# A two-layer attention and mixture-of-experts trunk: the input projection reads x before the norm's factor, GpSimd holds the empty scatters, and the heads' operands are split earlier and in three rows

## The reference, cut to what matters

```
h = rms_norm(x, norm1_gain);  z = h @ w_in          # columns q | k | v | u, 512 each
q, k = per-head rms_norm (8 heads of 64), rotary on the first 16 dims, q scaled by 1/8
att  = three causal dilated windows merged by their softmax denominators
pool = four channel groups: causal trailing mean of u over 2/4/8/16 positions minus u, a linear map, a scale
x = x + concat(att, pool) @ w_out
x = x + experts(rms_norm(x, norm2_gain))            # top-1 of 4 groups, top-2 of 4 experts in it
```

## Time and profile before

| | |
|---|---|
| median of 3 runs | 1663.27 us (1661.2 to 1667.27) |
| the profiled execution's own time | 1666.6 us |
| its span, first to last instruction | 1664.8 us |
| mean granted TensorE clock | 0.936 |
| PE / DVE / ACT / GpSimd busy | 1427.9 / 997.0 / 666.1 / 348.0 us |

### The profile page before, as it was taken

How to read it: one execution, slowest core, us unless ns; L and a number is a source line. 1 busy time by engine, 2 the same in 40 slices (tenths; PEclk the granted TensorE clock), 3 DMA queues, 4 the chain that set the end, 5 groups by cost and what they waited for, 6 DMA issues and landing times.

```text
span 1664.8 us, 24259 instructions
## 1 busy us (share of the span) xinstructions
PE 1427.9 (86%) x7323; PEld 1142.5 (69%) x7324; DVE 997.0 (60%) x1919; ACT 666.1 (40%) x1028; POOL 348.0 (21%) x204
## 2 busy tenths in 40 slices
PE   5999978998995699999299999699989938999981
PEld 4887868887784466666178788688968826666650
DVE  6777666664446666666467866756534475556560
ACT  4232145673211355555332313556611124555450
POOL 1000059002000123233510000950100011223324
PEclk9999988999998799999699999989999959999995
DMA  8100020000129599984770001100001665989937
GB/s 313 31 1 0 0 102 2 1 2 13 51 80 371 168 285 298 341 223 101 162 239 0 1 0 65 38 1 1 2 14 75 232 223 163 274 258 311 294 50 127
DMA packets 115873, 204.46 MB, mean 123 GB/s; under 512 B 9816, under 2 KB 76576, under 8 KB 115776
## 3 DMA queue, kind: packets, MB, share of 16 engines
q1 hardware_dynamic: 90976, 130.77, 22.9%
q0 software_dynamic: 19136, 53.67, 14.6%
q10 hardware_dynamic: 5664, 18.88, 2.9%
HBM read 169.72 MB, written 49.28 MB: 132 GB/s over the span
## 4 chain that ended last, share of the span: by engine, by line
PE 60%; DMA 14%; DVE 10%; issue 9%; ACT 4%; DVEq 2%; POOL 1%; ACTq 1%; SPq 0%; POOLq 0%; PEld 0%; PEldq 0%
PE ps L1501 18%; DMA out_x<-x_res,arena 11%; PE ps L1634 9%; PE ps L1481 9%; PE ps L1715 7%; PE ps L1587 7%; PE ps L1730 4%; PE ps L1561 2%; DMA big<-in_w_in 2%; PE ps L1563 1%; PE ps L1651 1%; DVE arena L1262 1%; DVEq L1372 1%; DVE xgT_lo L1376 1%; PE ps L1621 1%
## 5 line engine op out<-in xcount | busy, mean ns | idle before, releaser
L1367 DVE TENSOR_TENSOR gu_lo<-big,gu_hi 128x2048 fp32r<-128x2048 f32 x96 | 218.6, 2291 | 166.4 <-ACT gu_hi L892 133.0
L1481 PE MATMUL ps<-cst,arena 128*128 128x128 f32 x1226 | 183.2, 283 | 75.1 <-DVE arena L1019 32.9
L1481 PEld LDWEIGHTS ps<-cst,arena 128*128 128x128 f32 x1226 | 148.3, 145 | 124.7 <-DVE arena L1019 34.9
L1501 PE MATMUL ps<-w_in_hi,hT_hi 128*128 128x512 f32 x512 | 204.9, 400 | 12.8 <-DVE hT_lo L1037 10.0
L1501 PE MATMUL ps<-w_in_hi,hT_lo 128*128 128x512 f32 x512 | 201.3, 393 | 0.0
L1501 PE MATMUL ps<-w_in_lo,hT_hi 128*128 128x512 f32 x512 | 201.0, 393 | 0.0
L671 POOL DMA_INDIRECT x_res<-token_rows,row_tok x62 | 91.7, 1479 | 516.0 <-issue 308.7
L892 ACT ACTIVATE gu_hi<-big 128x2048 fp32r (+1 forms) x96 | 181.4, 1916 | 35.3 <-PE ps L1715 35.0
L1715 PE MATMUL ps<-gu_hi,xgT_hi 128*128 128x512 f32 x360 | 150.1, 417 | 23.6 <-DVE xgT_lo L1376 23.6
L1730 PE MATMUL ps<-big,arena 128*128 x360 | 163.8, 598 | 4.7 <-issue 4.7
L1156 DVE CUSTOM_DVE_ANT_0 arena<-ps,cst 128x128 f32<-128x128 f32 (+7 forms) x128 | 96.8, 756 | 102.7 <-PE ps L1563 102.2
(11 more groups left out here) (182 smaller groups left out, 2306.2 us busy)
## 6 DMA issues: line engine op xcount, KB each, us to landing
big<-in_w_gate SPq DMA_DIRECT2D x32, 1024.0 KB, 9.2
big<-in_w_up SPq DMA_DIRECT2D x32, 1024.0 KB, 13.9
big<-in_w_down SPq DMA_DIRECT2D x32, 1024.0 KB, 14.0
big<-in_w_in SPq DMA_DIRECT2D x14, 1024.0 KB, 10.1
big<-in_w_out SPq DMA_DIRECT2D x4, 2048.0 KB, 10.4
token_rows<-arena ACTq DMA_DIRECT2D x16, 512.0 KB, 3.2
out_x<-x_res ACTq DMA_DIRECT2D x16, 512.0 KB, 4.0
x_res<-out_x SPq DMA_DIRECT2D x8, 512.0 KB, 5.9
```

Source lines behind the costliest of these rows:

```text
L1367: ve.tensor_tensor(out=gu_lo[i], in0=raw, in1=gu_hi[i].bitcast(f32), op=ALU.subtract)\
L1481: ins = te.transpose(ps[:, bank + i // 4, (i % 4) * P:(i % 4 + 1) * P], src, ident)
L1501: ins = te.matmul(ps[:, 2 + 2 * par_ + i, :], a[par_][:, k, :], b[:, k, :], start=k == 0 and n == 0, stop=k == K - 1 and n == 2)
```

## The change

1. **Projection.** PE transposes x itself (`xr`) as soon as the block is loaded; xs, `norm_x_again` and the multiplication in `norm_x` go. r is kept for each block in st[:, 128 + t] and applied later: ACT's squares of q and k and its copies of v and u take it as a scale, and `norm_qk` multiplies it into its own factor. The order of the first steps changes in both layers: `gain1(0)` comes before `norm_x(0)`. All blocks are written out, not looped over.
2. **Scatters.** ACT no longer waits in its branches. GpSimd's `add_rows(j)` first waits for a new semaphore `may_add`, raised by one behind each `moe_down`, and by 15 for the spare ones: in layer 0 after ACT has split the first quarter of the next w_in and SP has raised `spare_may`, in layer 1 right after the last used block.
3. **Operands.** For the first head, q's high part and low part and the clearing of k_low[0] move into the last block of the projection; k's split is done for 896 and then 128 tokens. For the others, DVE's three instructions are spread over rows 1, 2 and 3. Buffers move so that this is free of conflicts.

```diff
@@ scatters
                 def add_rows(j):
+                    pool.wait_ge(may_add, j + 1)
                     pool.wait_ge(y0_ready, upto(l, BLOCKS, j + 1))
...
+                pool.wait_ge(may_clear, upto(l, 1, 1))
+                pool.sem_inc(s_passed, 1)
+                pool.sem_clear(may_add)
@@ ACT
             def square_x(l, t, par_):
                 a_.wait_ge(x_ready, upto(l, T, t + 1))
-                if not first(t):
-                    a_.wait_ge(xs_ready, upto(l, 2 * T, t))
-                    a_.wait_ge(xt_done, upto(l, 2 * T, t))
+                if t >= 2:
+                    a_.wait_ge(r_ready, upto(l, T, t - 1))
...
+                    if h and last(t, T):
+                        a_.wait_ge(t_evac, upto(l, 3 * T, T))
+                        q_top(0, 0)
                     a_.wait_ge(z_done, upto(l, 4 * T, 2 * n + 1))
-                    sc.activation(sqz, ps[:, 2 + 2 * par_, :].rearrange("p (h c) -> p h c", c=HD), ACT.Square)\
+                    a_.wait_ge(r_ready, upto(l, T, t + 1))
+                    sc.activation(sqz, ps[:, 2 + 2 * par_, :].rearrange("p (h c) -> p h c", c=HD), ACT.Square,
+                                  scale=st[:, 128 + t:129 + t])\
...
                     sc.activation(y[slot][:, 512:1024], ps[:, 5, :], ACT.Copy).then_inc(y1_ready, 1)
+                    a_.sem_inc(may_add, 1)
...
                     with a_.Else():
-                        a_.wait_ge(spare_may, upto(l, 1, 1))
                         a_.sem_inc(y1_ready, 1)
...
-                    in_high(l + 1, 0, [0])
+                    first_gain(l + 1)
+                    in_high(l + 1, 0)
+                    a_.wait_ge(spare_may, upto(l, 1, 1))
+                    a_.sem_inc(may_add, SPARE)
+                    a_.sem_inc(may_clear, 1)
                     square_x(l + 1, 0, 0)
-                    first_gain(l + 1)
-                    in_high(l + 1, 0, [1])
                     in_high(l + 1, 1)
@@ DVE
             def norm_x(l, t, par_):
                 dve.wait_ge(sd1, upto(l, T, t + 1))
-                r = st[:, 4 + par_:5 + par_]
-                rsqrt(st[:, par_:par_ + 1], st[:, 2 + par_:3 + par_], r, st[:, 6:7], 1.0 / D)
-                ve.tensor_copy(st[:, ds(128 + t, 1)], r)
-                ve.tensor_scalar(xs, xr[:, t, :], r, None, ALU.mult).then_inc(xs_ready, 1)
+                rsqrt(st[:, par_:par_ + 1], st[:, 2 + par_:3 + par_], st[:, 128 + t:129 + t], st[:, 6:7], 1.0 / D)
+                dve.sem_inc(r_ready, 1)
...
+            def first_q_low(l):
+                dve.wait_ge(q_high_in, upto(l, 2 * PAIRS, 1))
+                ve.tensor_tensor(out=q_parts[0][HD:P, :], in0=qT[0:HD, 0, :],
+                                 in1=q_parts[0][0:HD, :].bitcast(f32), op=ALU.subtract)
+                dve.wait_ge(z_done, upto(l, 4 * T, 4 * T - 2))
+                ve.memset(k_low[0][HD:P, :].bitcast(f32), 0.0)
...
+                if h and last(t, T):
+                    first_q_low(l)
+                if h == 0 and not last(t, T):
+                    norm_x(l, t + 1, 1 - par_)
...
+            gain1(0, 0, 0)
             norm_x(0, 0, 0)
-            in_low(0, 0, [0])
-            gain1(0, 0, 0)
-            in_low(0, 0, [1])
+            in_low(0, 0)
...
+                for n, c in enumerate((slice(0, SEQ - P), slice(SEQ - P, SEQ))):
+                    k_lower(0, 0, n + 1, c)
+                    ins = k_copy(0, 0, c)
+                ins.then_inc(staged, 1)
                 dve.wait_ge(tqk_done, upto(l, 3 * T, 3 * T))
-                ve.memset(k_low[0][HD:P, :].bitcast(f32), 0.0)
                 ve.memset(k_low[1][0:HD, :].bitcast(f32), 0.0)
-                q_and_k_low(0, 0, 0)
...
-                    if n == 3:
-                        q_and_k_low(p, 1, 2 * p + 1)
-                    if n == 11 and p < PAIRS - 1:
-                        q_and_k_low(p + 1, 0, 2 * p + 2)
+                    a, q = 1 - n // T, p + n // T
+                    if q < PAIRS:
+                        if n % T == 1:
+                            q_low(q, a, 2 * q + a)
+                        if n % T == 2:
+                            k_lower(q, a, 2 * q + a + 2)
+                        if n % T == 3:
+                            k_copy(q, a).then_inc(staged, 1)
...
                 with dve.If(l < DEPTH - 1):
-                    in_low(l + 1, 0, [0])
-                    norm_x(l + 1, 0, 0)
-                    in_low(l + 1, 0, [1])
+                    in_low(l + 1, 0)
                     dve.wait_ge(gain_in, upto(l + 1, 1, 1))
                     gain1(l + 1, 0, 0)
+                    norm_x(l + 1, 0, 0)
@@ PE
                 def xt(n):
-                    pe.wait_ge(xs_ready, upto(l, 2 * T, n + 1))
-                    transposes(0, cols(xs, K)).then_inc(xt_done, 1)
+                    if n < T:
+                        pe.wait_ge(x_ready, upto(l, T, n + 1))
+                    transposes(0, cols(xr[:, n % T, :], K)).then_inc(xt_done, 1)
```

More of the change, by code:

```diff
@@ L310, in trunk @@
         spare_may = sem("spare_may")
+        may_add = sem("may_add")
+        may_clear = sem("may_clear")
         gu_loaded = sem("gu_loaded")
@@ L395, in trunk @@
         SURE = (2 * SEQ // P - 1) // RING
+        SPARE = BLOCKS - 2 * SEQ // P
         def before(slot, m):
@@ L799, in _ @@
                 for h in range(2):
-                    steps(a_, T, lambda t, par_, m: in_act(t, par_, h), ch)
+                    for t in range(T):
+                        in_act(t, t % 2, h)
                     if h == 0:
@@ L1049, in in_low @@
                                      in1=w_in_hi[i % 2][:, c].bitcast(f32), op=ALU.subtract).then_inc(win_split, 1)
+            def first_q_low(l):
[4 more added lines that the diff above has]
+                ve.memset(k_low[0][HD:P, :].bitcast(f32), 0.0)
             def in_dve(l, t, par_, h):
                 n = h * T + t
-                if h == 0:
-                    if not last(t, T):
-                        norm_x(l, t + 1, 1 - par_)
-                    else:
-                        norm_x_again(l, 0)
-                elif not (first(t) or last(t, T)):
-                    norm_x_again(l, t + 1)
+                if h and last(t, T):
+                    first_q_low(l)
+                if h == 0 and not last(t, T):
+                    norm_x(l, t + 1, 1 - par_)
                 if h == 0 or not last(t, T):
@@ L1065, in in_dve @@
                 if h == 0 and last(t, T):
-                    norm_x_again(l, 1)
                     in_low(l, 3)
@@ L1120, in _, with k_lower, k_copy, q_low @@
                 ch.restart()
-                steps(dve, T, lambda t, par_, m: in_dve(l, t, par_, 0), ch, begun=True)
-                steps(dve, T, lambda t, par_, m: in_dve(l, t, par_, 1), ch)
-                def q_and_k_low(p, a, n):
+                for n in range(1, 2 * T):
+                    in_dve(l, n % T, n % 2, n // T)
+                def k_lower(p, a, n, c=slice(0, SEQ)):
+                    own = slice(HD * a, HD * (a + 1))
+                    dve.wait_ge(k_high_in, upto(l, 2 * PAIRS + 1, n))
+                    ve.tensor_tensor(out=k_low[a][own, c], in0=kT[own, p, c],
+                                     in1=k_high[a][own, c].bitcast(f32), op=ALU.subtract)
+                def k_copy(p, a, c=slice(0, SEQ)):
+                    own, other = slice(HD * a, HD * (a + 1)), slice(HD * (1 - a), HD * (2 - a))
+                    return ve.tensor_copy(k_high[a][other, c], kT[own, p, c])
+                def q_low(p, a, n):
                     own, other = slice(HD * a, HD * (a + 1)), slice(HD * (1 - a), HD * (2 - a))
@@ L1131, in q_and_k_low @@
                                      in1=q_parts[a][own, :].bitcast(f32), op=ALU.subtract)
-                    dve.wait_ge(k_high_in, upto(l, 2 * PAIRS + 1, n + 2))
-                    ve.tensor_tensor(out=k_low[a][own, :], in0=kT[own, p, :],
-                                     in1=k_high[a][own, :].bitcast(f32), op=ALU.subtract)
-                    ve.tensor_copy(k_high[a][other, :], kT[own, p, :]).then_inc(staged, 1)
+                for n, c in enumerate((slice(0, SEQ - P), slice(SEQ - P, SEQ))):
+                    k_lower(0, 0, n + 1, c)
+                    ins = k_copy(0, 0, c)
+                ins.then_inc(staged, 1)
                 dve.wait_ge(tqk_done, upto(l, 3 * T, 3 * T))
-                ve.memset(k_low[0][HD:P, :].bitcast(f32), 0.0)
                 ve.memset(k_low[1][0:HD, :].bitcast(f32), 0.0)
-                q_and_k_low(0, 0, 0)
                 dve.wait_ge(s_mask, 16)
@@ L1542, in _ @@
                 for h in range(2):
-                    steps(pe, T, lambda t, par_, m: in_pe(t, par_, h))
+                    for t in range(T):
+                        in_pe(t, t % 2, h)
                 turn(1, T - 1, (T - 1) % 2)
@@ L1774, in maybe_pe @@
                     with pe.Else():
+                        if not last(t, BLOCKS):
+                            pe.wait_ge(xtm_done, upto(l, BLOCKS, t + 1))
```

(3 more changed lines are left out.)

37 lines of the change are left out of this document (17 added, 20 removed).

## The result

The changed kernel takes 1650.84 us, the median of six runs (1639.09 to 1652.59); the kernel before took 1665.27 beside it. The ratio is 0.9887, with a 95% interval of 0.9855 to 0.9920. So it is faster: the medians differ by 14.4 us, and the ratio would make it 18.8. I forecast 35.3 us and a range of 1612 to 1646. The sign was right, and the measured time lies outside the range (by the ratio it would be 1646.5, at its edge). The profiled execution took 1649.49 us, 17.1 less than the profiled one of before.

A forecast was written before the change was run, and what follows sets the result against it. PE bounds the kernel, busy 86% of the span, so gains lie where it stands still or runs at 1.2 GHz. 3.6 + 1.7 + 14 + 12 + 5 - 1 = 35.3 us, from the median 1663.3 to 1628; range 1612 to 1646.

The forecast's parts named there:

- the splits in three rows: Attention heads: spreading DVE's splits makes PE's stalls shorter and keeps its clock up; 12 us, bounds 4 and 18.
- a rival with a chance of 0.06: Attention heads: each split pays its own wait for GpSimd, 19 us more and no gain in the rows; 1659 us.
- a third burst: Layer 1's heads: attention begins 6 us earlier against GpSimd, so another burst of splits falls into pooling; -2.0 us.
- 0.3 us a head: Eight other heads: the gain counted for each from spreading the splits, within the 15.8 us taken as 12.
- Start of layer 0: Projection's start: PE begins matmuls at 15.8 instead of 17.97 and block 1 follows earlier; 3.6 us, 4 at most.
- w_in, which I had named as a rival: Projection's start, both layers: PE still stands behind weights, so 3.6 and 5 us are lost; 1637 us, chance 0.08.
- Middle: Middle of the projection, both layers: dropping norm_x_again saves 0.86 us each; 1.7 us, bounds 1 and 2.5.
- Begin of attention: Both layers: scores come 6.1 us earlier and the clock stays at 1.00; 14 us, bounds 10.5 and 16.
- Between the layers: Passage to layer 1: ACT leaves without its 15.69 us wait, PE's matmuls begin 10 us earlier; 5 us, bounds 2 and 9.
- the pause of 6 us: Passage to layer 1: PE lacks work some 6 us before block 1, falls to 1.2 GHz and loses 2 us.
- GpSimd's wait: Scatters: one more wait for each costs 1 us over 45 used blocks, bounds 0 and 6.

The follow-up runs named there:

- the pieces: The changed kernel with GpSimd's split of the output weights cut into instructions of 1024 elements: 1624.49 us, ratio 0.9771; the same cut in the kernel before: 1662.49 us, 0.9974.

## Why the prediction was wrong

**The step that failed** is the one on the splits in three rows, and in it the sentence that DVE "does the same work", so that the end of the stretch "moves by no more than DVE's idle time in it". The work is not the same, because a split that meets one of GpSimd's instructions lasts until that one ends. I had the mechanism as a rival with a chance of 0.06, and sized it from the earlier trace rows at 2.07 us a split at most, since before no split met more than the tail of GpSimd's longest one; the copy in head 2 paid 8.26 - 0.69 = 7.57. So the two heads 2, where I had counted on 1.5 us, lost 18.2. For layer 1 I let a third burst fall into pooling, for 2 us, but I never asked which instruction of GpSimd each split would meet after attention had moved by 9.9 us and GpSimd by 3.8. GpSimd's order in attention is fixed and its instructions were in the trace of before; laying the heads' new times over it would have shown the 9 us subtraction under head 2. The instruction's length and its position were each varied, and both agree: the copy grows with the piece (1.76, 3.97, 8.27 us), and moving the long instruction away gives the same as cutting it (0.9777 and 0.9771). With it cut the kernel takes 1624.5 us, 3.5 from my forecast; that closeness is partly luck, since the pieces are worth 3 to 4 us in the kernel before too, and other terms were off both ways.

The rule could have been read before.'s split of k ends at 268.01, 1.08 us behind GpSimd's addition in the row below (266.93), and in all fourteen traces a split that outlasts such an instruction ends at the same distance behind its end: 1.08 us for a low part, 0.55 for a copy.

```profile
257.79 9.14 POOL L625 TENSOR_TENSOR big<-big 128x1024 f32<-128x1024 f32 x4 [0.18 <-POOL big L634]
```

One kind of GpSimd's instructions does not hold a split to its end: pooling's multiplication by 1 / win, a TENSOR_SCALAR. Before, it ran from 229.59 to 233.34, and the earlier trace rows's copy took 1.43 us inside it and was through at 232.12. A split inside it took between nothing and 0.8 us more than alone. Why it differs was not tried.

```profile
229.59 3.75 POOL L633 TENSOR_SCALAR big<-big 128x1023 f32<-128x1023 f32 x1
```

The Trainium skill, SBUF — State Buffer, section on the two separate sides, has this as a rule: VectorE and GpSimd share one pair of ports as an exclusive lock, and the one that starts first keeps it for its whole instruction, against a Vector operation in a two-port mode or with two SBUF inputs (the latter only where GpSimd's instruction reads SBUF). The traces agree for GpSimd's additions, subtractions and casts, with the copy that ends 0.55 us behind the 9.72 us subtraction, the low part that ends 1.1 us behind the cast, and masks that take 1.23 us beside 8.93. They do not agree for its TENSOR_SCALAR, inside which the copy of the earlier trace rows ended. In the prediction I had named another page of the Trainium skill, which gives no price.

**A second, smaller cause:** in the even heads q's low part stands behind `over_sum` in row 1 and delays the mask of row 4, so ACT's exponential of row 4, and behind that ACT's copy of row 3's transposed probabilities, for which PE waits (in head 2 of layer 0 that copy ends at 271.64, and PE goes on at 271.74). PE's pause in row 3 grows from 0.73 us, as it was before, to 1.66, and that pause goes either way: the next transposes took 1.06 us in some heads and 1.85 to 1.94 in others, at half the clock. It is the negative sum of heads 3 to 7 in the table (-1.5 and -3.2), where I had 0.3 us a head to gain. One row later the heads take 19.1 us again. In the prediction's terms it is the same step: q's low part was moved two rows forward, and I looked for its effect on row 4's `half_evac` alone.

**Point by point.** *Start of layer 0*: 3.0 for 3.6; PE started at 15.50 for 15.8, but behind w_in, which I had named as a rival. *Middle*: 0.9 and 0.9 for 1.7 together. *Begin of attention*: `staged` came 6.2 us earlier beyond the projection's share, where I had 6.1; undoing it cost 13 us for the 14 forecast, in part by way of the clock in later heads. *Three rows*: 13 us for 12 with the pieces, nothing with the long instructions, and some 4 in the kernel before with pieces. *Between the layers*: 3.9 for 5, by another way. Against the start of PE's last used down product (787.66, before 796.31) ACT was earlier by 7.9 us (its table load stands at 801.51), but PE was not. Timeline of PE:

```profile
816.38 1.96 PE L1502 MATMUL ps<-cst,x_res 128*128 128x128 f32 x8 [23.32 <-issue]
821.92 0.80 PE L1523 MATMUL ps<-w_in_hi,hT_hi 128*128 128x512 f32 x1 [3.58 <-DVE hT_lo L1043]
```

DVE waited 8.94 us for these transposes, while ACT had begun to square this block of x at 806.62, so that x was there: PE's own way through the empty blocks to the next layer ends last now. I had the first matmul 10 us earlier against the last used block; it was 0.8 against the start of that block's last product, and 2.5 against its end. The 3 us came behind it, since block 1 followed without the pause of 6 us that I expected. What PE does in the 23.3 us was not tried apart. *GpSimd's wait*: no cost is to be seen; ACT waited 112.5 us for scatters, 27 times, against the earlier trace rows. The 5.5 us behind the heads of layer 1 in the table were not traced to an edit. They come in jumps: 2.2 us up to the first expert blocks, 5.9 more up to 1468 (in the time of before), and 3.4 back at about 1590. The profiled pair differs by 17.1 us and the medians by 14.4, so some 3 us may be the scatter of single runs. The rest stays open.

## What to carry to other kernels

When a change moves a stage in time, lay its instructions over what the other engines do at the new time, the fixed order of GpSimd above all: a price read where two engines happened to meet only briefly is no price. Beside VectorE work that PE waits for, cut GpSimd's instructions to the length of a stall that can be borne, even though that makes GpSimd's sum longer. And look for pauses of PE that lie near the length at which its clock has gone both ways; a row more or less between two of them was worth 0.9 us a head here where the clock stayed up, and 2.5 to 4.1 where it fell.

## What the runs showed of the hardware that I had not expected

- A VectorE copy from SBUF to SBUF of 64x1024 takes 0.69 us alone and 8.26 beside a GpSimd instruction of 9.72; it ends 0.55 us behind that instruction and doesn't slow in proportion. Inside GpSimd's TENSOR_SCALAR of 3.75 us it took 1.43 and ended first.
- A subtraction of two SBUF inputs of the same size takes 1.22 us alone and 3.67 beside GpSimd's cast of 4.69; it ends 1.08 us behind it.
- A mask with one input in PSUM and one in SBUF, of 128x1024, takes 1.23 us beside GpSimd's instruction of 8.93, as it does without it.
- PE's clock fell to half behind a pause of 1.66 us in some heads and stayed up behind one of the same length in others (1.94 and 1.06 us for eight transposes); in the earlier trace rows it had stayed up behind 2.90.
- PE passed from its last used block to the next layer in 23.3 us with no work and no data outstanding that the profile shows; what it did was not tried apart.
